# Where the mixer convolution's norm, silu and split stand among the weight units, and VectorE's order at one step

## The reference, cut to what matters

```python
h = rms_norm(x, pre_mix_g[l])
z = h @ w_in[l]
za, zb, zc = z[..., :split_a], z[..., split_a:split_b], z[..., split_b:]
ya = spatial_gating(jax.nn.gelu(za, approximate=False), gate_ln_g[l], gate_ln_b[l], w_s[l], b_s[l])
yb = moba_attention(q, k, v)             # q, k, v from zb, 8 heads of 64, causal, ALiBi
yc = conformer_conv(zc, w_dw[l], b_dw[l], conv_gn_g[l], conv_gn_b[l])
y = jnp.concatenate([ya, yb, yc], axis=-1) @ w_out[l]
x = x + rms_norm(y, post_mix_g[l])
m = rms_norm(mem, mem_g[l])              # memory keys and values of the cross-attention
```

## Time and profile before

| | us |
|---|---|
| median of three runs | 768.32 |
| the runs | 767.16 to 768.35 |
| the profiled execution | 767.74 |
| its span, first to last instruction | 766.5 |
| busy in it: TensorE / VectorE / ScalarE / GpSimd | 756.8 / 580.8 / 447.5 / 73.3 |

### The profile page before, as it was taken

One profiled execution on the slowest core, in us unless ns is written; L12 is line 12 of the kernel. 1 busy time (PEld: TensorE's weight loads), 2 busy tenths in 40 slices (PEclk: granted clock), 3 DMA queues, 4 the chain that ended last, 5 costly groups with the idle time before them and its releaser, 6 DMA issues.

```text
span 766.5 us, 11109 instructions
## 1 busy us (share of the span) xinstructions
PE 756.8 (99%) x4276; PEld 651.1 (85%) x4276; DVE 580.8 (76%) x808; ACT 447.5 (58%) x673; POOL 73.3 (10%) x128
## 2 busy tenths in 40 slices
PE   8999999999999999999999999999999999999997
PEld 6998877888898888888899997789988888888885
DVE  5989999989796576776787998667758755665664
ACT  7666687775664444444474497467547644444453
POOL 5035720000200000000020001110001100000000
PEclk9999999999999999999999999999999999999999
DMA  9989998655477776866556554446434766666641
GB/s 355 398 280 353 329 346 306 229 184 163 139 222 217 243 239 208 281 189 198 184 169 214 167 164 149 147 161 206 146 99 138 219 194 193 192 192 192 189 168 55
DMA packets 77751, 161.29 MB, mean 210 GB/s; under 512 B 5170, under 2 KB 7538, under 8 KB 77699
## 3 DMA queue, kind: packets, MB, share of 16 engines
q1 hardware_dynamic: 76272, 157.31, 62.6%
q10 hardware_dynamic: 994, 2.79, 1.0%
q0 software_dynamic: 432, 0.49, 0.2%
HBM read 159.51 MB, written 1.05 MB: 209 GB/s over the span
## 4 chain that ended last, share of the span: by engine, by line
PE 94%; DVE 3%; ACT 2%; issue 1%; DMA 0%; DVEq 0%; ACTq 0%
PE bank L2058 18%; PE bank L2059 17%; PE bank L2060 17%; PE bank L2160 15%; PE bank L2163 8%; PE bank L2134 5%; PE bank L2071 2%; PE bank L2078 2%; PE bank L2073 2%; PE bank L2518 1%; PE bank L2091 1%; PE bank L2213 1%; PE bank L2334 1%; DVE lo_ring L1123 1%; PE bank L2258 1%
## 5 line engine op out<-in xcount | busy, mean ns | idle before, releaser
L1123 DVE TENSOR_TENSOR lo_ring<-raw_ring,hi_ring 128x1024 fp32r<-128x1024 f32 x247 | 302.6, 1231 | 135.7 <-ACT hi_ring L567 134.8
L567 ACT CAST hi_ring<-raw_ring 128x1024 fp32r<-128x1024 f32 x247 | 258.5, 1052 | 233.0 <-PE bank L2060 128.3
L2058 PE MATMUL bank<-hi_ring,branch_hi 128*128 128x512 f32 x352 | 138.5, 394 | 0.0
L2059 PE MATMUL bank<-lo_ring,branch_hi 128*128 128x512 f32 x352 | 137.2, 390 | 0.0
L2060 PE MATMUL bank<-hi_ring,branch_lo 128*128 128x512 f32 x352 | 137.0, 389 | 0.0
L2160 PE MATMUL bank<-h_hi_lo,hi_ring 128*128 128x512 f32 x512 | 128.1, 392 | 0.0
L2160 PEld LDWEIGHTS bank<-h_hi_lo,hi_ring 128*128 128x128 f32 x512 | 92.9, 189 | 17.2
L2060 PEld LDWEIGHTS bank<-hi_ring,branch_lo 128*128 128x128 f32 x352 | 66.1, 188 | 14.1
L2058 PEld LDWEIGHTS bank<-hi_ring,branch_hi 128*128 128x128 f32 x352 | 66.1, 188 | 13.9 <-issue 0.9
L2059 PEld LDWEIGHTS bank<-lo_ring,branch_hi 128*128 128x128 f32 x352 | 66.2, 188 | 13.0 <-issue 0.2
L2163 PEld LDWEIGHTS bank<-h_hi_lo,lo_ring 128*128 128x128 f32 x512 | 69.8, 190 | 5.0
(11 more groups left out here) (341 smaller groups left out, 1162.8 us busy)
## 6 DMA issues: line engine op xcount, KB each, us to landing
raw_ring<-in_w_ff SPq DMA_DIRECT2D x128, 512.0 KB, 3.7
raw_ring<-in_w_in SPq DMA_DIRECT2D x63, 512.0 KB, 4.5
raw_ring<-in_w_out SPq DMA_DIRECT2D x16, 512.0 KB, 3.3
raw_ring<-in_w_xkv SPq DMA_DIRECT2D x16, 512.0 KB, 3.6
mem_v<-in_w_ada SPq DMA_DIRECT2D x13, 512.0 KB, 5.0
mem_k<-in_w_ada SPq DMA_DIRECT2D x11, 512.0 KB, 5.2
ada_ring<-in_w_ada SPq DMA_DIRECT2D x8, 512.0 KB, 7.3
raw_ring<-in_w_branch SPq DMA_DIRECT2D x8, 512.0 KB, 3.4
```

The costliest lines, as they stand in the source:

```text
L567: act.copy(m.hi[:, m.slot(u)], m.raw[:, m.slot(u)]).then_inc(s.hi_done, 1)
L1123: dve.tensor_tensor(m.lo[:, m.slot(u)], m.raw[:, m.slot(u)], as_f32(m.hi[:, m.slot(u)]), ALU.subtract).then_inc(s.lo_done, 1)
L2058: pe.matmul(out, a_hi, b_hi, start=start, stop=False, skip_group_check=True)
L2059: pe.matmul(out, a_hi, b_lo, start=False, stop=False, skip_group_check=True)
```

## The change

On VectorE at step 12 the low parts of pairs 0 and 1 come first, then the last three taps, then the gate. Before, the taps stood one unit earlier, ahead of the low parts. `conv_norm` moves from step 14 to 15 on TensorE and VectorE, `conv_silu` and the scaling from 16 to 17, the silu on ScalarE from 17 to 18, the split from 18 to 19. `conv_center` and the square stay at step 13. GpSimd's code is the same and follows the variance's semaphore.

```diff
@@ act_program, follow
-        if step == 17:
+        if step == 18:
             act.wait_ge(s.conv_scaled, 1)
...
@@ dve_program, follow
         if step == 12:
             attended_lo(a, 0, 7, 0)
             attended_lo(a, 1, 6, 1)
+            conv_taps(3)
+            gate_mix()
         if step in (13, 15):
             g = 2 + (step - 13) // 2
             attended_lo(a, g, pair_bank(g), g)
-        if step == 12:
-            gate_mix()
...
-        if step == 14:
+        if step == 15:
             dve.wait_ge(s.conv_var_ps, 1)
...
-        if step == 16:
+        if step == 17:
             dve.wait_ge(s.conv_scale_ps, 1)
...
-        if step == 18:
+        if step == 19:
             dve.wait_ge(s.conv_act, 1)
             split_to_branch(m.conv_y2, 6, 2, s.yc)
...
-        conv_taps((4, 3, 0, 0)[j])
+        conv_taps((4, 0, 0, 0)[j])
```

## The result

| | before | after |
|---|---|---|
| median, us | 768.16 (6 runs, 766.89 to 768.57) | 770.27 (6 runs, 769.88 to 771.56) |
| ratio to before | 1 | 1.0029, 95% interval 1.0019 to 1.0039 |
| the profiled execution (its span) | 767.74 (766.5) | 771.56 (770.3) |

The changed kernel is 2.1 us slower. Its median lies inside the range of 768.0 to 771.4, 0.6 us above the forecast of 769.7. The ratio lies on the other side of the prediction's bound of 0.2%, with an interval that begins just under it (1.0019). By that bound the likeliest class (0.53) did not come; the slower one (0.42) did.

What follows compares the result with a forecast made beforehand. TensorE was taken to bound the kernel. Gains 0.39 + 0.50 = 0.89 us against losses 2.23 + 0.10 = 2.33 us gave net +1.4 us, 769.7 us against the median of 768.32, range 768.0 to 771.4.

Steps and rivals of the forecast that it cites:

- the prediction's bound of 0.2%: Whole kernel: about 0.2% (1.5 us) is what a measurement can tell from no change.
- the likeliest class (0.53): Whole kernel: time the same as before, not measurably different; chance 0.53, against slower 0.42 and faster 0.05.
- TensorE alone sets the time: Whole kernel: TensorE is busy for 99% of the span; changes on other engines count only where it waits.
- Part 1: VectorE's low parts ahead of the taps: pair 3's transposes start after 0.23 instead of 0.62 us, gaining 0.39 us.
- Part 2: conv_norm moved from between units 0 and 1 to between units 1 and 2: a gain of 0.50 us.
- Covers: Delayed taps, gate, variance copy, GpSimd steps and ring low parts finish before TensorE needs them, so cost nothing.
- Part 3: Silu and split one unit later: a 5.12 us chain behind unit 4 makes TensorE wait 2.23 us at unit 6.
- The restart of 0.10: After the wait at unit 6, the first two matmuls are 0.33 instead of 0.23 us apart: 0.10 us, bounds 0 and 0.4.
- The table load's price: ScalarE, between unit 4's cast and the silu: 1.32 us by the row, against the skill's 2.66 us.
- The first rival: ScalarE's table load runs ahead of the cast; wait at unit 6 falls to 0.95, net about +0.1, 768.4 us; chance 0.12.
- The clock: Rival: the wait at unit 6 also lowers TensorE's clock, costing up to 2.7 us, time up to 772.4; chance 0.08.
- signs of being wrong: No wait at unit 6, granted clock under 1.00 between 500 and 515, late pair 3 transposes, or waits at unit 2 or conv_silu.

Runs made afterwards that it cites:

- silu_late_alone: Kernel before with only the silu moved to step 18 and its split to step 19; median 771.89 us, ratio 1.0049.
- table_early: Changed kernel plus a silu of one element per partition into scratch on ScalarE at step 17; median 768.71 us, ratio 1.0004.
- silu_at_19: Changed kernel with the silu one more step later, at step 19; median 774.46 us, ratio 1.0077.
- filler: Changed kernel with nine unread matmuls of 512 columns on TensorE ahead of the wait before unit 6; median 770.16 us, ratio 1.0026.

## Why the prediction was right or wrong, point by point

- **TensorE alone sets the time**: right. What moved on VectorE, ScalarE and GpSimd counted only through TensorE's waits, and behind the stretch every profile takes the same 255.3 to 255.4 us. The medians go the way of the local stretches, but for silu_late_alone, whose profiled execution is its shortest.
- **Part 1, a gain of 0.39 us**: right in its place (483.20 to 483.43) but incomplete as a part of its own. Alone it only moves the wait on to conv_norm. In the sum it stands because part 2 takes that next wait away, which the prediction did not say.
- **Part 2, a gain of 0.50 us**: right, 0.53 alone. Both gains together were 0.97 instead of 0.89; about 0.05 of the rest is that attend2 follows the transposes by 0.75 us where they did not wait (483.43 to 484.18 in the changed kernel, 483.04 to 483.84 before).
- **Covers**: right. The variance's copy, GpSimd's steps and the gate brought no wait.
- **Part 3, a wait of 2.23 us**: right. Unit 6 starts 2.46 us behind unit 5's last matmul instead of 0.23, with a chain of 5.12 us. The restart of 0.10 was right too (507.73 to 508.06).
- **The table load's price**: 1.32 us by the row, and table_early takes 1.27 us off the wait with it. "ScalarE: Activation LUTs" of the Trainium skill, "What ACT_TABLE_LOAD costs", adds a drain of 1380 ns; in table_early the small silu starts at 501.21, directly behind the load's end at 501.20. The rows of this case show no such drain, and they decide here.
- **The first rival's net**: its own terms, 0.95 + 0.10 - 0.89, make +0.16 and 768.5, not +0.1 and 768.4; that moves neither the forecast nor the range.
- **The clock, left at nothing**: this is the step that failed, a term of the sum that was mis-sized. A granted clock under 1.00 between 500 and 515 was among the prediction's own signs of being wrong, and it came. The mechanism was named as a rival at 0.08 and argued away with the tail of the trace: 0.91 of the last 6.5 us read as a clock that outlasts some 4 us of idling, so a wait of 2.2 us seemed safe. One such row shows one execution, and it is no bound: in silu_at_19 the grant fell about 2.0 us into the wait. In the changed kernel's profile the grant fell behind a wait of 2.07 us, after TensorE had resumed, and eight matmuls of unit 6 ran at 0.43 us: 1.6 us. The price was inside the bound of 2.7. By the listed clocks it came in four of eleven executions. By an estimate from these, with four elevenths of 1.6 us, the sum of 1.4 becomes a mean of about 2.0, beside measured medians of +2.1 and +2.6 us. "TensorE: Matmul & The Clock Gate" of the Trainium skill, "Why this matters for your kernels", warns of longer idle gaps than this one. In two of the three profiles with a wait of 2.1 us the grant fell to 0.50 behind it all the same; in the third (silu_late_alone) it did not. For this kernel the measurement decides.
- **Range and chances**: the range left out most of the clock's price and held for the median, in part by luck: the clock fell in a minority of the executions, and the longest one (771.56) lies above its upper end. The likeliest class was missed, with a forecast only 0.1 us under the bound. That the clock alone pushed the median over it is not shown: the filler, whose clock held, lies over it too (1.0026, +1.85 us).

What stays open: why the clock falls in some executions behind the same wait and holds in others, and how often; the listed clocks and the profiles show both, no run here sets it. Open too is why filler and silu_late_alone lie above what their stretches give.

## What to carry to other kernels

Moving a step one slot later on one engine can change what it queues behind on another: read, for each engine, what stands ahead of the moved instruction and which event lets that go, and count how many units of work the waiter has left beside it. Removing one wait pays only if the next one in the same chain has slack, so cost neighbouring edits together and alone. A wait on TensorE of 2 us inside a busy stretch is to be priced with the clock in it, here as a chance of 1.6 us on top, unless something fills or shortens it (the wait of 0.80 us was without that cost).

## What the runs showed of the hardware that was not expected

- The granted clock fell about 1 us after TensorE had resumed from a wait of 2.07 us (508.7 after 507.73) and rose again near 512.0; in another execution it fell about 0.6 us after the resumption (507.9 after 507.27).
- Nine matmuls whose result nobody reads, put into the same gap, kept it at 1.00, and the local stretch was 1.61 us shorter than without them.
- A wait of 0.80 us left the clock at 1.00 and so did one of 2.06 us (silu_late_alone); one of 4.78 us lost it within the wait, about 2.0 us in. In the tail of before it held for some 4 us behind the last matmul.
